# Table building moved into the projection, convolution and state space part merged into one stage, output weights split in the first mixing step

## What is computed

```python
h = rms_norm(x, g_mix);  z = h @ w_in                # 1024 -> 1536
u = z[:, :512] * sigmoid(z[:, 512:1024])             # convolution branch
y_conv = silu(layer_norm(causal_depthwise_conv31(u) + conv_b))
s = z[:, 1024:]                                      # 32 groups of 16 channels
a = exp(lam * exp(log_dt)); b = (a - 1) / lam * B    # complex, 64 states a group
h_t = a * h_{t-1} + b @ s_t;  y = gelu(Re(C @ h_t) + d * s_t)
y_ssm = y * sigmoid(y @ glu_w + glu_b)
x = x + concat(rms_norm(y_conv, g), rms_norm(y_ssm, g)) @ w_out
x = rms_norm(x + moe(rms_norm(x, g_ffn)), g_final)   # 4 groups of 8 experts, top 1 then top 2
```

## Time and profile before

| | |
|---|---|
| Time, median of 3 runs | 1968.36 us (1967.24 to 1974.44) |
| Time of the profiled execution | 1972.62 us |
| Its span, first to last instruction | 1971.1 us |
| PE busy | 1661.4 us (84%) |
| DVE, ACT, POOL busy | 1103.8, 800.4, 599.4 us |
| Mean granted clock of TensorE | 0.911 |
| DMA | 403.90 MB, mean 205 GB/s |

### The profile page before, as it was taken

One profiled execution on the slowest core, in us unless ns is written; L12 is line 12 of the kernel. 1 busy time (PEld: TensorE's weight loads), 2 busy tenths in 40 slices (PEclk: granted clock), 3 DMA queues, 4 the chain that ended last, 5 costly groups with the idle time before them and its releaser, 6 DMA issues. The chain is left out here.

```text
span 1971.1 us, 33308 instructions
## 1 busy us (share of the span) xinstructions
PE 1661.4 (84%) x11179; PEld 1513.0 (77%) x11180; DVE 1103.8 (56%) x1640; ACT 800.4 (41%) x968; POOL 599.4 (30%) x891
## 2 busy tenths in 40 slices
PE   7999995686386699999918999999999999999970
PEld 7999995654264588878718989989999888899870
DVE  6533513633364566766563655673566888556555
ACT  4211200223021433334123555573555777565543
POOL 0777773000144323654432121212212212122120
PEclk9999995679688799899958999999999999999995
DMA  8542317424985332341273887895788999888858
GB/s 274 180 158 85 121 51 160 104 85 145 278 252 154 106 117 86 118 108 65 86 278 111 275 291 228 275 358 163 237 280 277 358 367 385 268 264 271 277 148 351
DMA packets 171644, 403.90 MB, mean 205 GB/s; under 512 B 76606, under 2 KB 109504, under 8 KB 143552
## 3 DMA queue, kind: packets, MB, share of 16 engines
q1 hardware_dynamic: 144992, 336.25, 48.3%
q0 software_dynamic: 20080, 58.34, 12.1%
q10 hardware_dynamic: 6512, 8.51, 1.6%
HBM read 313.92 MB, written 89.13 MB: 204 GB/s over the span
## 5 line engine op out<-in xcount | busy, mean ns | idle before, releaser
L1686 DVE TENSOR_TENSOR expert_lo<-expert_raw,expert_hi 128x2048 fp32r<-128x2048 f32 x192 | 430.6, 2285 | 46.6 <-ACT expert_hi L1682 46.4
L1682 ACT CAST expert_hi<-expert_raw 128x2048 fp32r<-128x2048 f32 x192 | 361.8, 1910 | 18.0 <-DMA expert_raw<-in_experts 9.8
L570 PE MATMUL proj_p_z<-proj_x_hi,proj_w_hi 128*128 128x256 f32 x768 | 220.3, 287 | 14.0 <-DVE proj_x_lo L499 14.0
L571 PE MATMUL proj_p_z<-proj_x_lo,proj_w_hi 128*128 128x256 f32 x768 | 218.5, 285 | 0.0
L572 PE MATMUL proj_p_z<-proj_x_hi,proj_w_lo 128*128 128x256 f32 x768 | 218.4, 284 | 0.0
L2086 PE MATMUL moe_p_g0u<-expert_hi,moe_xh 128*128 128x256 f32 x736 | 210.6, 286 | 1.5 <-DVE moe_xl L1999 1.5
L2088 PE MATMUL moe_p_g0u<-expert_lo,moe_xh 128*128 128x256 f32 x736 | 206.4, 280 | 0.0
L2087 PE MATMUL moe_p_g0u<-expert_hi,moe_xl 128*128 128x256 f32 x736 | 206.3, 280 | 0.0
L2101 PE MATMUL moe_p_y<-expert_hi,moe_hh 128*128 128x512 f32 x368 | 153.3, 417 | 12.6 <-DVE moe_hl L2010 12.6
L570 PEld LDWEIGHTS proj_p_z<-proj_x_hi,proj_w_hi 128*128 128x128 f32 x768 | 148.7, 194 | 14.4 <-issue 14.0
L1928 POOL DMA_INDIRECT residual<-moe_y,moe_ids_s x46 | 78.3, 1701 | 259.2 <-ACT moe_y L1955 251.7
(11 more groups left out here) (422 smaller groups left out, 4153.0 us busy)
## 6 DMA issues: line engine op xcount, KB each, us to landing
expert_raw<-in_experts SPq DMA_DIRECT2D x192, 1024.0 KB, 7.8
ffn_input<-mix_h SPq DMA_DIRECT2D x17, 512.0 KB, 4.1
proj_x_sb<-in_x SPq DMA_DIRECT2D x8, 1024.0 KB, 7.0
mix_x_sb<-in_x SPq DMA_DIRECT2D x16, 512.0 KB, 5.6
residual<-mix_x SPq DMA_DIRECT2D x16, 512.0 KB, 2.7
out<-final_x SPq DMA_DIRECT2D x16, 512.0 KB, 6.1
proj_x_raw<-in_x_turned SPq DMA_DIRECT2D x7, 1024.0 KB, 4.8
proj_w_raw<-in_w_in SPq DMA_DIRECT2D x8, 768.0 KB, 7.6
```

What stands on the lines that cost most here:

```text
L570: nc.tensor.matmul(o, whi, x_hi[:, half, c], start=start, stop=False)
L571: nc.tensor.matmul(o, whi, x_lo[:, half, c], start=False, stop=False)
L1682: self.nc.scalar.copy(self.hi[:, u], self.raw[:, u]).then_inc(self.hi_done, 1)
L1686: tensor_tensor(self.lo[:, u], self.raw[:, u], self.hi[:, u].bitcast(FP32), ALU.subtract).then_inc(self.lo_done, 1)
```

## The change

1. **Tables in the projection.** The factor list (`table_factors`) runs on DVE after its first step. B and C come laid out from the host, without the transposition on PE, into the room of `w_raw`, whose weights have been split by then. The expansion works on two groups at a time (16 pairs), in two buffers; three pairs a step from the third step on. PE makes the table products of one group (`table_products`) behind each unit of the projection, into the one bank that is free, `p_t`; ACT copies them, DVE adds d to lag 0 (`skip_lag`), SP stores four tables a pair.
2. **One stage for convolution and state space part** (`convolution_and_ssm`). 16 slots m: PE makes bank m of the convolution, the drive of pair m+1 and the output of pair m. Blocks have four groups (two slots), so that they are loaded in eight times 21 DMAs. The PSUM banks are two for the convolution, four for drives and two for outputs. The loops are written out. One meeting of the engines goes.
3. **Output weights in mixing.** `w_out` and `glu_w` are loaded in ten pieces of 512 KB into `x2` and `h` within the first mixing step, rounded on ACT (`split_hi`) and subtracted on DVE (`split_lo`), and the first output products wait for them one by one.

The same tables, products and results are computed. The core of the diff:

```diff
+            sp.wait_ge(w_lo_done, 6)
+            sp.dma_start(b_raw.rearrange("p i g c -> p (i g c)"), b_in).then_inc(bc_in, 16)
+            sp.dma_start(c_cols.rearrange("p i g c -> p (i g c)"), c_in).then_inc(bc_in, 16)
+            sp.dma_start(d_cols[:, :], ssm_d).then_inc(bc_in, 16)
             s_v = scratch["s"].rearrange("(c p) s k -> s p c k", p=P)
+
+            def store_pair(m, parity):
+                of_pair = lambda name: scratch[name].rearrange("p (u g) m -> u p g m", g=PAIR)[m]
+                sp.wait_ge(tab_copied, PAIR * m + PAIR)
+                sp.dma_start(of_pair("w12"), w12).then_inc(st_pair, 16)
+                sp.dma_start(of_pair("o2"), o2[:, :, :]).then_inc(st_pair, 16)
+                sp.dma_start(of_pair("o1"), o1[parity][:, :, 1:NP].rearrange("p g j c -> p g (j c)")).then_inc(st_pair, 16)
+                sp.wait_ge(kern_ready, PAIR * m + PAIR)
+                sp.dma_start(of_pair("kernel"), kern[:, :, :]).then_inc(st_pair, 16)
...
                 sp.dma_start(s_v[n], s_out[:, :, :]).then_inc(s_stored, 16)
+                for k in range(pairs):
+                    store_pair((n - FIRST) * PER_STEP + k, (half + k) % 2)
                 sp.wait_ge(u_done, n * CT + CT)
...
+            def copy_tables(g, m):
+
+                act.wait_ge(products_done, PAIR * m + g + 1)
+                wait(act, st_pair, 64 * m)
+                nc.scalar.copy(w12[:, g], p_t[:, 0:2 * P])
+                nc.scalar.copy(o2[:, g], p_t[:, 2 * P:3 * P])
+                nc.scalar.copy(kern[:, g, (T8 - 1) * GC:], p_t[0:GC, 3 * P:4 * P]).then_inc(tab_copied, 1)
...
-                    gate(n, j)
-                    if j == 1 and more is not None:
+                for j in range(UNITS):
+                    if j >= 2:
+                        gate(n, j - 2)
+                    if j == 3 and more is not None:
                         spread_factor(n + 1, 1 - half)
-
...
+                    dve.wait_ge(products_done, PAIR * m - PAIR)
+                    dve.wait_ge(st_pair, 64 * m - 64)
+                cc = [c_cols[:, i] for i in range(2)]
+                for k, (to, fac_re, fac_im, ar, ai, lags) in enumerate((
+                        (v[parity], in_re, in_im, bb[:, 0], bb[:, 1], T8), (o1[parity], out_re, out_im, *cc, NP))):
+                    vstep = Chain(dve, v_own, m * 4 + 2 * k)
+                    second = by_lag(vt[:, 0:PAIR * lags * GC], lags)
+                    for fac, a, out in ((fac_re, ar, to), (fac_im, ai, second)):
+                        f = of_pair(fac, "p (u g) j -> p u g j")[:, :, 0:lags]
+                        vstep(V.tensor_tensor(out, f.unsqueeze(3).broadcast_to([P, PAIR, lags, GC]),
+                                              of_pair(a, "p (u g) c -> p u g c").unsqueeze(2).broadcast_to([P, PAIR, lags, GC]),
+                                              ALU.mult))
+                    V.tensor_tensor(to, to, second, ALU.add).then_inc(v_ready, 1)
...
+            def skip_lag(m, g):
+
+                dve.wait_ge(tab_copied, PAIR * m + g + 1)
+                lag0 = kern[:, g, (T8 - 1) * GC:T8 * GC]
+                V.scalar_tensor_tensor(out=lag0, in0=ident[0:GC, 0:GC], scalar=d_cols[:, bass.ds(PAIR * m + g, 1)], in1=lag0,
+                                       op0=ALU.mult, op1=ALU.add).then_inc(kern_ready, 1)
+
...
+
+                def prepare(k):
+                    m = (n - FIRST) * PER_STEP + k
+                    if k < pairs and (not isinstance(m, int) or m + 1 < PAIRS_OF_GROUPS):
+                        expand(m + 1, (half + k + 1) % 2)
+
+                def skip_lags(k):
+                    if k < pairs:
+                        for g in range(PAIR):
+                            skip_lag((n - FIRST) * PER_STEP + k, g)
...
                 if more:
                     low(n + 1, 1 - half)
                     dve.wait_ge(spread, n + 1)
                     factors(n + 1)
-                for j in (0, 1, 2, 3):
-                    scaled(n, half, j)
-                for j in (4, 5):
-                    glu(n, j - 4)
-                    scaled(n, half, j)
+                scaled(n, half, 0)
+                prepare(0)
+                scaled(n, half, 1)
+                scaled(n, half, 2)
+                skip_lags(0)
+                prepare(1)
+                scaled(n, half, 3)
+                glu(n, 0)
+                scaled(n, half, 4)
+                skip_lags(1)
+                prepare(2)
+                glu(n, 1)
+                scaled(n, half, 5)
                 for j in (2, 3):
                     glu(n, j)
-
-            body(0, 0, False)
-            body(1, 1, True)
+                skip_lags(2)
+
+            body(0, 0, False, 0)
+            table_factors()
+            body(1, 1, True, 0)
...
+            def table_products(m, g, parity):
+                pe.wait_ge(v_ready, 2 * m + 2)
+                wait(pe, tab_copied, PAIR * m + g)
+                flat = lambda ap: ap.rearrange("p j c -> p (j c)")
+                nc.tensor.matmul(p_t[:, 0:2 * P], flat(v[parity][:, g]), eye_turn[:, :], start=True, stop=True)
+                nc.tensor.matmul(p_t[0:GC, 3 * P:4 * P], v[parity][:, g, 0, :], flat(o1[parity][:, g, 0:T8, :]),
+                                 start=True, stop=True)
+                nc.tensor.matmul(p_t[:, 2 * P:3 * P], eye_turn[:, P:2 * P], flat(o1[parity][:, g, 1:NP, :]),
+                                 start=True, stop=True).then_inc(products_done, 1)
+
+            def products(n, half, more, pairs):
                 pe.wait_ge(lo_done, n + 2)
                 for j, blocks in enumerate(units):
...
+            def load_in(n):
+                half = n % 2
+                wait(sp, y_done, (n - 1) * PR)
                 for s in range(T8):
                     rows = slice((T8 - 1 - s) * GC, (T8 - s) * GC)
                     sp.dma_start(inp[rows, half], s_v[n][s]).then_inc(in_loaded[half], 16)
-                sp.dma_start(w12[:, half], whole("w12")).then_inc(in_loaded[half], 16)
...
+                sp.dma_start(w12[:, half], whole("w12", n)).then_inc(in_loaded[half], 16)
+
...
+            load_u(0)
+            load_column(nc, sp, bias[:, :], conv_b).then_inc(b_in, 16)
+            load_in(0)
+            sp.wait_ge(tables_st, 16 * TB)
+            load_toep(0)
+            load_rest(0)
+            load_u(1)
+            load_in(1)
+            load_rest(1)
+            load_toep(1)
+            load_u(2)
+            for n in range(2, BLOCKS):
+                load_in(n)
+                load_rest(n)
+                if n in (3, 5):
+                    load_toep((n + 1) // 2)
+                if n == 3:
+                    load_u(3)
...
+            pe.wait_ge(ut_cleared, 1)
+            drive_of(0)
+            for m in range(SLOTS):
+                bank(m)
+                if m + 1 < SLOTS:
+                    drive_of(m + 1)
+                out_of(m)
...
+            clear_toep(V, 0, 0, FAST).then_inc(cleared_dve, 1)
+            turn(0)
+            states(0)
+            turn(1)
+            for m in range(1, SLOTS):
+                states(m)
+                if m % BANKS == 1 and m > 1:
+                    t = m // BANKS
+                    turn_back(t - 1)
+                    if t + 1 < CT:
+                        turn(t + 1)
+            turn_back(CT - 1)
...
+            act.wait_ge(b_in, 16)
+            for m in range(SLOTS):
+                copy_bank(m)
+                if m % BANKS == 2 and m > 2:
+                    finish(m // BANKS - 1)
+                copy_y(m)
...
+            def load_piece(c):
+                wait(sp, w_lo_done, c - NAMED + 1)
...
+            sp.dma_start(branch_gain[:, :], g_branch).then_inc(cols_in, 16)
+            for c in range(NAMED):
+                load_piece(c)
...
+            for c in range(NAMED, PIECES):
+                load_piece(c)
...
+            def split_hi(pieces):
+                for c in pieces:
+                    hi, _, part = piece(c)
+                    act.wait_ge(raw_in[c % NAMED], 16 * (c // NAMED + 1))
+                    nc.scalar.activation(hi, part, ACT.Copy, scale=1.0 if c < 2 else branch_gain[:, c - 2:c - 1]).then_inc(w_hi_done, 1)
+
...
             def body(n, par):
+                if first(n):
+                    split_hi(range(0, 3))
                 if not last_step(n):
...
                     front2(n, par)
+                    if first(n):
+                        split_hi(range(5, 7))
                 if not first(n):
...
+                if first(n):
+                    split_hi(range(7, PIECES))
                 if not first(n):
                     logit(n * 2 - 2, 0)
                     tile_square(n * 2 - 1, 1)
...
             def body(n, par):
+                if first(n):
+                    split_lo(range(0, 3))
                 if not last_step(n):
...
                 if chosen_in(n):
                     choose((n - 3) // 2)
+                if first(n):
```

(5 more changed lines are left out.)

805 lines of the change are left out of this document (316 added, 489 removed).

## The result

| | before | after |
|---|---|---|
| Time, median of 4 runs | 1969.87 us | 1887.56 us (1880.8 to 1895.12) |
| Ratio | | 0.958 (0.956 to 0.961) |
| Profiled execution, its span | 1972.62, 1971.1 us | 1895.12, 1893.7 us |
| PE busy | 1661.4 us (84%) | 1640.9 us (87%) |
| Mean granted clock | 0.911 | 0.924 |

What follows compares the result with a forecast made beforehand. PE bounds the projection; latency and ordering bound the two stages after it, with no engine full. 1972.6 + 51.2 - 324.4 + 189.2 + 4.5 = 1893.1, median 4.2 below: 1889 us, range 1855 to 1930.

Steps and rivals of the forecast that it cites:

- Table products, +38.4: Projection: three table products for each of 32 groups at 1.20 us a group, all on PE's path, +38.4 us.
- the slack of 1 to 2 us on ACT: Projection: ACT's table copies, waiting for the previous pair's stores, have 1 to 2 us left, so they cost zero.
- Stall, 14.3: Projection's second step: PE waits 13.3 us for DVE's factors behind the list, plus 1 us low clock; bounds 6 and 30.
- End of the projection, -1.5: Projection's end: only the store of u counts, no longer POOL's last turn store; -1.5 us, ends 0 and -3.
- The joint stage, 189: Joint stage replacing 324.4 us: start 15, two low-clock slots 31, fourteen slots of 9.3, tail 13; 189 us.
- Its other bound, 11.2: Joint stage: upper end for a slot, 11.2 us, which is 150 us at the old DMA share of 0.83.
- First mixing step, 4.5: First mixing step: loading, rounding and subtracting ten weight pieces delays it 4.5 us; ends 0 and 12.
- They have 10 us to spare: First mixing step: SP sends the next step's loads only after the last piece, with 10 us to spare.
- (1): Joint stage: transfers rule at 11.2 us a slot, stage 216 us, kernel 1916 us; chance 0.16.
- (2): Joint stage: low clock never lifts, slots of 15.5 + 1 us, stage 292 us, kernel 1992 us; chance 0.04.
- (3): Projection: DVE's table steps wait for POOL and starve PE, 1959 us, chance 0.03; partial form about 1911, chance 0.15.
- (4): Joint stage and projection: better overlap, 8.4 us a slot and a stall of 6, kernel 1868 us; chance 0.12.

Runs made afterwards that it cites:

- experiment 1: Kernel after the change with each group's three table products made twice: 1925.93 us, 38.4 more than the kernel after.
- nine traces: Traces of kernels that leave the kernel after's joint stage alone: that stage takes 177.6 to 184.7 us, 180.6 in the mean.
- experiment 4: Kernel after with first mixing step edited: conv_in load earlier; pieces split elsewhere; both; both plus y_in load earlier: 1883.4, 1886.1, 1881.3, 1881.3 us.
- experiment 3: Kernel after with GpSimd's turn tables held back until DVE has made the list of table factors: 1881.74 us.
- experiments 2: Kernel after with the factor list in two parts behind later row factors, and table products from the third step's last third: 1869.77 us.
- both edits together: Kernel after with conv_in sent before the last seven weight pieces and the pieces rounded and subtracted in other places, first mixing step: 1881.3 us.

## Why the prediction was right, step by step

- **Table products, +38.4.** Twice them cost 37.9. PE's last product of the projection moved from 300.66 to 354.33, 53.7 us; less the stall and 0.9 us by which the second step began later, 36 us are theirs. The forecast lies between this and the 39.2 of experiment 1. No PE wait for tables or copies from the third step on: the slack of 1 to 2 us on ACT was enough.
- **Stall, 14.3.** 15.1 and 1.9 for the low clock (3.8 us at half the pace): 17.0. The chain of the estimate held, with errors that cancel in part. Contention with POOL on the list was 8.4 us, not 6, all of it in its first 21 operations; the split and row factors behind it took 5.4 and not 7.7, since the operations of POOL beside the row factors were of 0.25 to 0.34 us, where they had been of 0.62 to 0.80, and nothing waited for ACT; it began 1.0 later. The low clock was under-priced by half.
- **End of the projection, -1.5.** It is -4.4: 10.5 us lay between PE's last product and the next stage before, 6.1 after. The old end was POOL's store of the turn tables, issued 2.9 us behind PE's last product, with the next stage 7.7 us after that issue; the new one is that of u, issued 1.7 us behind PE, with the next stage 4.4 us after it. From issue to landing they took 4.9 and 2.9 us. The estimate looked at when the stores were sent and not at how long each takes to land, and its lower end was -3. Some 1.3 us between landing and next stage no run explains. Sum of the stage +49.2, predicted +51.2.
- **The joint stage, 189.** In the first trace: start 16.1 us (15; its own parts, 12.7 and nine loads at 3.67 for eight, add up to 16.8), two slots 24.6 (31), fourteen of 9.36 (9.3), tail 13.0 (13), together the 184.7; over nine traces 180.6. The step that failed by most is the low clock: I let it last through both slots, and it ended about 390, with the first: that took 15.6 (15.5), the second 9.0. Here the first trace is a good one: in the other eight the second slot took 7.9 to 15.4 us, the longer ones with a wait of PE for POOL of up to 5.3 us and a clock of 0.77 to 0.88, so that over the nine it is 11.7. The slot was right in size and in what bounds it: 8.8 in the mean of nine with the Toeplitz packets, 7.8 without, where PE alone had been counted at 8.05. Its other bound, 11.2, never came near.
- **First mixing step, 4.5.** Output products 7.6 later, the first residual store 8.9. Two statements were wrong. "They have 10 us to spare" for SP's loads: sent at 578.25, conv_in was awaited, and y_in too once POOL came to it earlier (experiment 4). And seven pieces "between the other steps" were not free: an ACT operation of 1.1 us ahead of each step of a chain moves it, and so do subtractions beside POOL (2.81 and 3.25 us for its next two cube operations, 1.89 and 2.36 before). Of the 12.2 us that the mixing stage lost, 8.9 stand before the first residual store, 1.7 in the eight steady steps (290.0 for 288.3, clock 0.92 for 0.93), and 1.6 behind them, which no run explains. Run again, the same kernel lost 7.1, since the steady steps took 283.8.

The three stages were off by -2.0, -4.5 and +8.6 (12.2 + 0.9 - 4.5), which nearly cancel: 1893.1 for the execution, 1895.12 measured, 1889 and 1887.56 for the medians. That agreement is closer than the steps deserve; the spread of the joint stage alone is 7 us, and by its mean of nine traces the second term would be 8.6 too high, not 4.5.

**The rivals.** (1) Transfers at 11.2 us a slot: not seen, though the transfers do set the slot, at 8.8 in the mean. (2) The low clock that never lifts: PE idled 2.3 to 6.6 us in three places and the clock was below 1.00 only in the stretches around them (0.90 and 0.63 in the rows shown). As a rule of the Trainium skill (TensorE: Matmul & The Clock Gate, section "HAM oscillation — how this bites in real kernels") phases broken by DMA waits can each start at the low clock; the rows agree for the four starts in this stage, and show that it stayed a cost at the starts. (3) The table steps starved by POOL: PE had no wait there, and of the list 8.4 us were lost, not 40; experiment 3 showed the mechanism at one pair (1.51 us for 0.43), where POOL's longest operations met it. The Trainium skill (SBUF — State Buffer, section "SBUF: two separate sides") says that the loser of the shared port waits for the whole instruction; the list agrees, 0.29 us became 0.85 to 1.33 beside POOL operations of 0.74 to 1.29 us, and became 0.29 again when POOL was held. What kept the price small is that POOL's operations are mostly short or waiting for its own stores, and that DVE's delay has to outlast its slack before PE feels it. (4) The better overlap, 1868, needed what experiments 2 and 4 then did by hand.

## What to carry to other kernels

When work is moved under a busy engine, price the queue in which its preparation stands: here the moved products cost what they should, and a list of 18 us ahead of one urgent operation cost 17 us more, of which a split of the list gave back 16.5. In a trace the longest wait at a late point isn't its only cause when another chain ends within a microsecond or two; only both edits together showed it. And when stages are joined to hide transfers, count packets beside bytes: 5% of the bytes were 30% of the packets, and without them a slot took 7.8 us and not 8.8.

## What the hardware showed that was not expected

- One kernel's stage takes 177.6 to 184.7 us over nine traces with the same instructions in it; PE's waits for w12 were 24.3 to 29.9 us in them, and the three slowest have the three longest (28.0 to 29.9); and the eight steady mixing steps take 281.2 to 290.0 us in them, at a granted clock of 0.96 to 0.92. Gains under some 5 us are read from the stage, not from the whole time.
- Eight loads of 256 KB in packets of some 127 bytes cost twelve slots 11.9 us in the mean (9.5 to 15.6 over the nine traces); SP took 8.17 and 8.37 us to issue four of them where eight loads of 64 KB took 3.7.
- Small DVE operations beside POOL ones are late by up to about a whole POOL operation: 0.29 us against 0.85 to 1.33 for 128x128, and 12.2 us for the 18 operations of the powers of a, which take 4.8 alone.
